# Sums of weight blocks by VectorE, or by adding loads on GpSimd's queue

## What is computed

```python
        h = rmsnorm(x, norm_g[layer, 1]) * (1 + sc2) + sh2
        x = x + g2 * (jnp.square(jax.nn.relu(h @ mlp_w1[layer])) @ mlp_w2[layer])
```

## Time and profile before

| | us |
|---|---|
| median of 3 runs | 1569.2 |
| lowest and highest | 1568.63, 1569.4 |
| span of the profiled execution | 1567.7 |
| TensorE busy in it | 1546.4 |
| VectorE busy | 989.9 |
| ScalarE busy | 625.7 |
| GpSimd busy | 487.8 |

### The profile page before, as it was taken

How to read it: one execution, slowest core, us unless ns; L and a number is a source line. 1 busy time by engine, 2 the same in 40 slices (tenths; PEclk the granted TensorE clock), 3 DMA queues, 4 the chain that set the end, 5 groups by cost and what they waited for, 6 DMA issues and landing times.

```text
span 1567.7 us, 28794 instructions
## 1 busy us (share of the span) xinstructions
PE 1546.4 (99%) x11994; PEld 1513.1 (97%) x11994; DVE 989.9 (63%) x1831; ACT 625.7 (40%) x1152; POOL 487.8 (31%) x350
## 2 busy tenths in 40 slices
PE   8999999999999999999999999999999999999998
PEld 7999999999999999999999999999999999999998
DVE  5348678675774755565555888773675755556555
ACT  5323333344432344234235534652443334523443
POOL 0233313314222343143235253101333344324431
PEclk9999999999999999999999999999999999999999
DMA  9454333313243334344253121001221232223212
GB/s 330 154 180 151 116 114 123 101 55 108 81 151 116 124 124 139 116 135 149 95 161 134 35 81 61 28 2 54 81 81 55 67 108 68 82 68 102 74 54 82
DMA packets 133410, 162.23 MB, mean 103 GB/s; under 512 B 4640, under 2 KB 108064, under 8 KB 133280
## 3 DMA queue, kind: packets, MB, share of 16 engines
q1 hardware_dynamic: 132048, 159.34, 31.5%
q10 hardware_dynamic: 1232, 1.05, 0.2%
HBM read 156.44 MB, written 3.93 MB: 102 GB/s over the span
## 4 chain that ended last, share of the span: by engine, by line
PE 90%; DVE 6%; ACT 2%; issue 1%; DMA 0%; POOL 0%; DVEq 0%; ACTq 0%
PE ps L665 59%; PE ps L1092 19%; PE ps L784 3%; PE ps L1284 2%; PE ps L1232 1%; DVE ps L1915 1%; PE ps L921 1%; PE ps L954 1%; DVE hL L1926 1%; PE ps L870 1%; DVE ps L1905 1%; PE ps L950 1%; DVE amx L2512 1%; ACT wH L1328 1%; PE ps L1259 1%
## 5 line engine op out<-in xcount | busy, mean ns | idle before, releaser
L1840 POOL TENSOR_TENSOR wL<-raw,wH 128x512 fp32r<-128x512 f32 x212 | 314.6, 1509 | 709.5 <-ACT wH L1328 514.7
L665 PE MATMUL ps<-fH,wH 128*128 128x320 f32 x1024 | 318.5, 311 | 0.2 <-DVE fL L2298 0.2
L665 PE MATMUL ps<-fL,wH 128*128 128x320 f32 x1024 | 316.3, 309 | 0.0
L665 PE MATMUL ps<-fH,wL 128*128 128x320 f32 x1024 | 316.3, 309 | 0.0
L1876 DVE SCALAR_TENSOR_TENSOR xT<-ps,modT,xT 128x192 f32<-128x192 f32 (+1 forms) x456 | 183.3, 434 | 192.0 <-PE ps L665 190.1
L1840 POOL TENSOR_TENSOR wL<-raw_high,wH 128x512 fp32r<-128x512 f32 x124 | 164.2, 1349 | 338.5 <-ACT wH L1351 209.6
L665 PE MATMUL ps<-hH,wH 128*128 128x320 f32 x704 | 221.1, 314 | 1.9 <-DVE hL L1926 1.3
L665 PE MATMUL ps<-hH,wL 128*128 128x320 f32 x704 | 217.5, 309 | 0.0
L665 PE MATMUL ps<-hL,wH 128*128 128x320 f32 x704 | 217.5, 309 | 0.0
L665 PEld LDWEIGHTS ps<-fH,wH 128*128 128x128 f32 x1024 | 192.3, 188 | 3.4 <-DVE xT L1876 1.2
L665 PEld LDWEIGHTS ps<-fL,wH 128*128 128x128 f32 x1024 | 192.3, 188 | 0.1
(11 more groups left out here) (271 smaller groups left out, 3095.4 us busy)
## 6 DMA issues: line engine op xcount, KB each, us to landing
ada<-in_ada_w SPq DMA_DIRECT2D x40, 1024.0 KB, 5.3
raw<-in_mlp_w SPq DMA_DIRECT2D x64, 512.0 KB, 3.7
raw_high<-in_mlp_w SPq DMA_DIRECT2D x64, 512.0 KB, 3.8
raw<-in_even_w_in SPq DMA_DIRECT2D x28, 512.0 KB, 5.9
pre_w<-in_ada_w SPq DMA_DIRECT2D x16, 512.0 KB, 8.9
raw<-in_odd_w_qkv SPq DMA_DIRECT2D x10, 512.0 KB, 3.5
raw<-in_even_w_out SPq DMA_DIRECT2D x8, 512.0 KB, 3.5
raw<-in_odd_w_o SPq DMA_DIRECT2D x6, 512.0 KB, 3.4
```

What stands on the lines that cost most here:

```text
L665: last = nc.tensor.matmul(ps[:, bank, 0:width], a_, b_, start=(k == 0 and p_ == 0), stop=(k == nk - 1 and p_ == 2))
L1840: last = nc.gpsimd.tensor_tensor(wL[:, at % 4, cs], raw(t)[:, j, cs], wH[:, at % 4, cs].bitcast(F32), ALU.subtract)
```

## The change

The four DVE sums of a Winograd cycle go. In their place stand loads that add to what lies in the buffer (`accum_op=ALU.add`), issued from GpSimd's queue, which read the weight block from `mlp_w1` once more. Since a load can only add, T1 to T4 become plain sums, and the signs move to S1, S4 and to a few of the combining operations, whose number and sizes stay. T1 becomes B11 + B12, T2 is B11 + B12 + B22, T3 is B12 + B22 made in place in `raw_high`, T4 is T2 + B21.

- SP issues two more loads of B11 in each Winograd cycle, into `t1_raw` and `t24_raw` (`t_first`), between the loads of tile 0 and tile 1 of `mlp_w1`. In the first Winograd cycle of a layer they wait for `s_ready`.
- GpSimd issues four adding loads after the low part of the last block of the cycle before (`first_sums`), each behind a wait; the third waits until the second has landed. A fifth, T4's, follows B11's low part and waits for T2's low part (`last_sum`).
- T2 and T4 share `t24_raw`. The half of `raw_high` with B12 is free only after T3's low part.

```diff
                         load_tile(first_tile + 4 * c + b, k8(mlp_w1[layer], 512 * c + 256 * b))
+                        if c >= PLAIN and b == 0:
+                            t_first(c)
...
+                def t_first(c):
+
+                    s, src = WINO * layer + c - PLAIN, k8(mlp_w1[layer], 512 * c)[0]
+                    if s % WINO == 0:
+                        sp.wait_ge(s_ready, 4 * layer + 4)
+                    if s:
+                        wait_low(sp, "p", s - 1, T1)
+                    sp.dma_start(t1_raw[:].rearrange("p (k n) -> p k n", n=256), src).then_inc(t1_in, 16)
+                    if s:
+                        wait_low(sp, "p", s - 1, T4)
+                    sp.dma_start(t24_raw[:].rearrange("p (k n) -> p k n", n=256), src).then_inc(t24_in, 16)
...
+            def add_block(s, i, out, q, done, landed):
...
+                pool.wait_ge(*landed)
+                nc.gpsimd.dma_start(out.rearrange("p (k n) -> p k n", n=256), src.rearrange("(k p) n -> p k n", p=P),
+                                    accum_op=ALU.add).then_inc(done, 16)
+
+            def first_sums(s):
+
+                t = (T_MLP0, T_MLP1)[s // WINO] + 4 * (PLAIN + s % WINO) + 1
+                add_block(s, T1, t_raw[T1], 2, t1_added, (t1_in, 16 * (s + 1)))
+                add_block(s, T2, t_raw[T2], 2, t24_added, (t24_in, 16 * (s + 1)))
+                add_block(s, T2, t_raw[T2], 3, t24_added, (t24_added, 48 * s + 16))
+                add_block(s, T3, t_raw[T3], 3, t3_added, (raw_landed(t, 0), 16 * (RAW_AT[t][1] + 1)))
+
+            def last_sum(s):
+
+                wait_low(pool, "p", s, T2)
+                add_block(s, T4, t_raw[T4], 1, t24_added, (t24_added, 48 * s + 32))
...
                 lo(key)
+                if key in SUMS_AT:
+                    first_sums(SUMS_AT[key])
+                if key[0] == "p" and key[2] == B11:
+                    last_sum(key[1])
...
-                        for n, i in zip((6, 7, 8, 9), SUM_ORDER):
-                            after[n] = after.get(n, []) + [lambda i=i: t_sums(s_next, (i,))]
                         after[11] = [lambda: t_lo(s_next, T2)]
```

More of the change, by code:

```diff
@@ L97 @@
 B11, T2, B21, T3, T1, T4, B22 = range(7)
-T_ORDER, SUM_ORDER = (T2, T3, T1, T4), (T3, T1, T2, T4)
+T_ORDER = (T2, T3, T1, T4)
 BLOCKS = []
@@ L322, in hybrid_step @@
         s_raw = {1: s1_raw, 2: s2_raw, 3: s3_raw, 4: s4_raw}
-        t3_raw, t2_raw, t4_raw = (nc.alloc_sbuf_tensor_at(f"t{n}_raw", [P, 1024], F32, offset=norm_buffers + 4096 * j)
-                                  for j, n in enumerate((3, 2, 4)))
+        t24_raw = nc.alloc_sbuf_tensor_at("t24_raw", [P, 1024], F32, offset=norm_buffers)
         here[0] = arena
@@ L367, in weights @@
             return [w[:, BLOCK_AT[key] % 4, :].rearrange("p (k n) -> p k n", n=n) for w in (wH, wL)]
-        t_raw = {T1: t1_raw, T2: t2_raw, T3: t3_raw, T4: t4_raw}
+        t_raw = {T1: t1_raw[:], T2: t24_raw[:], T3: raw_high[:, 0, :], T4: t24_raw[:]}
         s_hi = {1: hH[:, 0:4, 0:HALF], 2: s23[:, 0, 0], 3: s23[:, 1, 0], 4: s4[:, 0]}
@@ L480, in wait_raw_free, with t_summed @@
                 s, odd = WINO_OF(t)
-                engine.wait_ge(t_sum, 4 * s + 4)
-                if (odd, j) != (1, 0):
-                    wait_low(engine, "p", s, (B11, B21, None, B22)[2 * odd + j])
+                wait_low(engine, "p", s, (B11, B21, T3, B22)[2 * odd + j])
+        def t_summed(s, i):
+            return {T1: (t1_added, 16 * (s + 1)), T2: (t24_added, 48 * s + 32), T3: (t3_added, 16 * (s + 1)),
+                    T4: (t24_added, 48 * s + 48)}[i]
         block = ctx.enter_context(nc.Block())
@@ L1344, in split_product @@
                 if i in T_ORDER:
-                    act.wait_ge(t_sum, 4 * s + SUM_ORDER.index(i) + 1)
-                    src = t_raw[i][:]
+                    act.wait_ge(*t_summed(s, i))
+                    src = t_raw[i]
                 else:
@@ L1854, in rope_tables @@
                 last.then_inc(tab_done, 1)
+            def add_block(s, i, out, q, done, landed):
+                layer, c = s // WINO, PLAIN + s % WINO
+                src = mlp_w1[layer, 512 * (q % 2):512 * (q % 2 + 1), 512 * c + 256 * (q // 2):512 * c + 256 * (q // 2) + 256]
+                pool.wait_ge(*landed)
[10 more added lines that the diff above has]
+                add_block(s, T4, t_raw[T4], 1, t24_added, (t24_added, 48 * s + 32))
+            SUMS_AT = {(t0_ + 4 * c_ - 1, 1): WINO * layer_ + c_ - PLAIN for layer_, t0_ in enumerate((T_MLP0, T_MLP1))
+                       for c_ in range(PLAIN, CYCLES)}
             for key in POOL_LO:
@@ L2332, in s_low @@
                     nc.vector.tensor_tensor(s_lo[i], s_raw[i][:], s_hi[i].bitcast(F32), ALU.subtract).then_inc(s_ready, 1)
[L2334 to L2354, removed]
                 def t_lo(s, i):
@@ L2359, in t_lo, with combine, result @@
                     dve.wait_ge(wh_done, at + 1)
-                    nc.vector.tensor_tensor(wL[:, at % 4, :], t_raw[i][:], wH[:, at % 4, :].bitcast(F32),
+                    nc.vector.tensor_tensor(wL[:, at % 4, :], t_raw[i], wH[:, at % 4, :].bitcast(F32),
                                             ALU.subtract).then_inc(t_low, 1)
-                def combine(g, bank, m, add, out, done, at):
+                def combine(g, bank, m, add, out, done, at, op=ALU.add):
                     dve.wait_ge(acc_full, g + at + m)
-                    nc.vector.tensor_tensor(out, ps[:, bank + m, 0:HALF], add[:, m, :], ALU.add).then_inc(done, 1)
-                def result(s, g, n, bank, add, at):
+                    nc.vector.tensor_tensor(out, ps[:, bank + m, 0:HALF], add[:, m, :], op).then_inc(done, 1)
+                def result(s, g, n, bank, add, at, op=ALU.add):
                     if 8 * s + n > 3:
                         dve.wait_ge(fsq_done, 8 * s + n - 3)
-                    combine(g, bank, n % 2, add, fr[:, n % 4, :], c_done, at)
+                    combine(g, bank, n % 2, add, fr[:, n % 4, :], c_done, at, op)
                 def winograd(c):
```

11 lines of the change are left out of this document (6 added, 5 removed).

## The result

| | before | after |
|---|---|---|
| median of 4 runs each, us | 1568.91 | 1592.86 |
| lowest and highest | 1568.63, 1569.4 | 1591.71, 1593.55 |
| ratio of after to before | | 1.0152 (95% interval 1.0139 to 1.0164) |
| span of the profiled execution | 1567.7 | 1589.9 |

Lines have moved: TensorE's MLP line L665 is L682 after, `winograd` L1092 is L1109, `update` L1921, `t_lo` L2383, `s_low` L2377, ACT's split L1368, GpSimd's low part L1857. L1878 is the adding load, L603 and L606 are SP's loads into `t1_raw` and `t24_raw`. Experiments shift them by a few more.

What follows compares the result with a forecast made beforehand. TensorE, busy 1546.4 of 1567.7 us, was taken as the bound, helped or hurt only where it waits. 1567.7 + 21.4 (layer starts) + 0.5 (ten other cycles) = 1589.6 profiled, stated as 1590 us; range 1569 to 1660.

Steps and rivals of the forecast that it cites:

- What goes: 48 sums on VectorE in 12 Winograd cycles, 58.3 us of its work; off the path, so worth 0.
- Start of the chain: First Winograd cycle of a layer: after `s_ready` and a 5.3 us load, `t24_raw` is loaded at 528.0, layer 1 1228.1.
- The pair: T2's two adding loads in series at a layer's first Winograd cycle: 8.9 us each, 17.8 together.
- Waits: TensorE at each layer's first Winograd cycle: 10.1 us in layer 0, 11.3 in layer 1, together 21.4.
- The other ten cycles: Winograd cycles not first in a layer: 1 us of slack in layer 0; 0.1 us each in layer 1, 0.5 together.
- the rule of 2.9 us: T2 must be there 2.9 us before TensorE starts Winograd: update 12, low part, ACT's split and handing over.
- The volume: 84 extra loads of 512 KB over 12 cycles bring the DMA share to some 0.64; the volume as such costs 0.
- Slower than any row: Rival, 25%: beyond 18.8 us for the pair all ten other cycles pay too; at 12 us each, 1660 us.
- at 10 or more the waits recur in every cycle: Sign, landing of an adding load: near 9 us the forecast, near 4 the fast rival, 10 or more waits every cycle.
- As fast as plain ones: The fast rival, 15%: adding loads take up to 4.0 us each, the pair 8.0; 1571 us, no measurable change.
- The point from which it decides: Adding-load time up to which the fast rival holds: 4.5 us each, for a sum of 3.1 us.
- Faster: Rival, 3%: VectorE relieved of 58.3 us makes the kernel faster, 1567 us.

Runs made afterwards that it cites:

- e6_nosums: Kernel before, with its VectorE sums cut to 16 of 1024 columns in the ten cycles that are not the first of a layer; 1569.23 us, ratio 1.0001.
- e1_order: Kernel after, with T2's two adding loads ahead of T1's in GpSimd's queue; 1587.99 us, ratio 1.0121 to the kernel before.
- e3_plain: Kernel after, with the 60 loads of GpSimd's queue made plain, without the addition; 1582.99 us, ratio 1.0089 to the kernel before.
- after_again: Kernel after, unaltered, run and profiled a second time; 1592.56 us, ratio 1.0151 to the kernel before.
- e4_third: Kernel after, with B22 added a second time into T2 in all 12 cycles, a third adding load in the chain; 1673.08 us, ratio 1.0658.
- e7_spread: e2_early with SP's loads in a layer's first Winograd cycle reordered: half of raw_high, t24_raw, other half, t1_raw; 1570.23 us, ratio 1.0011 to the kernel before.
- e5_fill: Kernel after, with 60 idle matmuls on TensorE ahead of the first Winograd product of each layer; 1590.68 us, ratio 1.014 to the kernel before.
- e2_early: e1_order with t24_raw's load ahead of t1_raw's, waiting only for the first low part of S; 1575.38 us, ratio 1.0038 to the kernel before.

## Why the prediction was right

I had forecast 1590 us; 1592.9 was measured, in the direction and by the mechanism predicted, at the place predicted. (My sum gave 1591.1 on the scale of the medians; the 1590 was that of the profiled span, 1589.6, rounded.) Step by step:

- **What goes is worth 0: right.** `e6_nosums` shows it directly for ten of the twelve cycles. VectorE's busy time fell by 50.9 us, not 58.3; some other rows grew: the `t_lo` of T3 takes 1.74 us on average where all `t_lo` took 1.22 before, and the one at 549.28, with GpSimd's low part beside it, 3.21.
- **Start of the chain: right.** The `s_low` of S take 1.47 us each once B11's low part has moved away, as I had worked out. With the 1.6 us by which that execution ran ahead, T2's first adding load starts at 527.1 + 1.6 = 528.7, where I said 528.0. Two misses nearly cancel in it. The plain load takes 4.40 us, not the 5.3 that I had taken, and T1's adding load is issued just ahead: with handing over 1.6 us on the chain, where I had called it no term because I had T1's copy land 1.6 us before T2's.
- **The pair: right in layer 0 by two misses that cancel.** Predicted 8.9 + 8.9 = 17.8; measured 11.2 + 6.3 = 17.5 in layer 0 and 9.1 + 6.3, with 0.3 between them, in layer 1. I had taken the most crowded row for both trips. The first was dearer than that in layer 0, because T1's adding load stood ahead of it and SP's loads beside it, as `e1_order` and `e3_plain` show by taking the first or the addition away; the second had nothing ahead of it. So the value was near by luck, and "each 8.9" was no property of an adding load: that is 6.3 us with nothing ahead and up to 11.2 behind and beside others.
- **Waits: 21.4 predicted, 20.5 measured** (10.1 and 11.3 against 10.7 and 9.8).
- **The missed term: the clock, 3.3 us** (4.6 in `after_again`). My sum counted a wait as its own length only. With 0.9 us less of waits and 0.5 less in the ten other cycles it accounts for the distance between my sum, 1591.1, and 1592.9.
- **The other ten cycles: right, with more slack.** I had 1 us of slack in layer 0 and 0.1 over in layer 1, 0.5 us in all; the measured cost is 0. Cycle 3 of layer 0, GpSimd's and ACT's timelines:

```profile
582.73 2.57 POOL L1878 DMA_DIRECT2D t_raw<-in_mlp_w  x2
593.00 1.27 POOL L1878 DMA_DIRECT2D t_raw<-in_mlp_w  x1 [7.70 <-DMA t_raw<-in_mlp_w]
```

```profile
600.90 1.06 ACT L1368 ACTIVATE wH<-t_raw 128x1024 fp32r<-128x1024 f32 x1 [16.12 <-DMA t_raw<-in_mlp_w]
```

TensorE starts Winograd at 606.00 here, so by the rule of 2.9 us T2 had to be there at 603.1; it was there at 600.9, 2.2 us ahead. The pair took 16.9 us (from 584.0, behind T1's issue of 1.28, to 600.9). In cycle 3 of layer 1 it took 15.2 and T2 was there at 1307.65 for a date of 1312.65 - 2.9, 2.1 us ahead, where I had it 0.1 late. `e4_third` found about the same from the other side.

- **The volume costs nothing: right.** `e7_spread` moves all of it within 0.1% of the time of before. From 1200 to 1520 us the kernel after has a DMA share of 0.61, where I had 0.64.
- **The rivals.** "Slower than any row" was right only on the crowded first trip (11.18), and the ten cycles did not fall; `e4_third` shows that they would have, from some 2.2 us more. So my sign "at 10 or more the waits recur in every cycle" did not hold for a single first trip, and the median of 7.1 us lay between the signs that I had given for the forecast and for the fast rival. "As fast as plain ones" is out: 6.2 us is the fastest of the 48 landings in `t_raw`, where plain ones from GpSimd have 4.0 at best. (The point from which it decides is 4.3 us each by my own sum; the 4.5 that I gave makes 3.8 us, not 3.1.) The page "DMA: Bandwidth & Descriptors" of the Trainium skill (section "Anatomy of one DMA — SWDGE (gpsimd) path") gave 3.2 us, or 4.4 for twice the bytes; the trace does not agree, with 5.0 plain and 7.1 adding at the median. The 3.7 us that I had held against the 3.2 were those of SP's queue. "Faster" is out by `e6_nosums`.

## What to carry to other kernels

Moving an elementwise sum into adding loads trades work on an engine, which may be free, for latency in series: count the trips between the event that frees the buffer and the date on which the bound engine needs the result, and price each trip with all that the same event releases. Before giving such a change up, look at what its first load truly waits for, and move the uninvolved loads away from it: here a wait for one event instead of four, with three of SP's loads and T1's adding load reordered, turned 1.5% into 0.1%. Put the load that is waited for ahead of the others in GpSimd's queue. And where TensorE waits several microseconds, add a clock term behind the wait, here 1.6 to 3.0 us for each wait of 4 to 11 us in the kernel after, `e1_order` and `e3_plain`.

## What the runs showed of the hardware that I had not expected

- An adding load of 512 KB takes 6.2 us at least and 7.1 at the median, the same load plain from GpSimd 4.0 and 5.0, from SP into `raw` 3.9 at the median. It needs 528 packets instead of 144, and a packet takes 0.133 x 16 x 1589.9 / 31680 = 0.107 us of an engine's time against 0.058 on SP's queue (0.332 x 16 x 1589.9 / 144720).
- The place in GpSimd's queue shows in the trip. T3's adding load, issued right behind one other, takes 8.7 us at the median (8.2 at least); in `e1_order`, where it stands behind two, 12.0 (10.8 at least). T2's second, at the head of them, takes 6.2 to 6.4 at the layer starts.
- Its issue holds GpSimd: these groups of after give the mean of one in ns behind the comma, 1382 and 1842; with the plain loads of `e3_plain` it is 763 and 751.

```profile
L1878 POOL DMA_DIRECT2D t_raw<-in_mlp_w x48 | 62.3, 1382 | 167.6 <-DMA t_raw<-in_mlp_w 113.9 <-DVE wL L2383 53.2 <-issue 0.4
...
L1878 POOL DMA_DIRECT2D raw_high<-in_mlp_w x12 | 22.1, 1842 | 0.0
```

- A wait of TensorE costs again behind it, and not in proportion to its length. Waits of 9.8 and 10.7 us cost another 1.6 and 1.7 us of lower clock, those of 8.5 and 10.8 in `after_again` 2.4 and 2.2, those of 4.0 and 5.4 in `e3_plain` 3.0 and 2.5. In `e5_fill` a wait of 1.94 us, with the same matmuls behind it, cost 1.8 (5.28 us for 3.52), while one of 0.93 us in layer 1 (24.86 for 24.64) cost 0.2. In `e2_early` one of 2.6 us cost 1.8 and one of 1.7 us 0.2 (3.76 for 3.52). In `e4_third` waits cost up to 2.9 us (6.41 for 3.52), and it is open why some cost more than others.
